# The operand stage of two memory attentions and of a latent attention put in another order

## The reference, cut to what matters

```python
def memory_xattn(h, mem_h, wq, wk, wv, wo):      # h: 512 x 1024, mem_h: 256 x 1024; 4 heads of 256
    q, k, v = h @ wq, mem_h @ wk, mem_h @ wv     # h = rmsnorm(x, xa_ln), mem_h = rmsnorm(mem, xa_mem_ln)
    p = softmax(q k^T * 256 ** -0.5)
    return (p @ v) @ wo

def _mla_queries(a_q, q_a_norm, w_uq, q_norm, rope):                 # a_q: 512 x 256
    q = (_rms_norm(a_q, q_a_norm) @ w_uq).reshape(B, L, 16, 96)
    q = _rms_norm(q, q_norm)                                         # per token and head
    return concatenate([q[..., :64], _rope_2d(q[..., 64:], rope)])

def _mla_keys_values(a_kv, kv_a_norm, w_ukv, k_norm, rope):          # 512 tokens of x, 256 of the context
    kv = (_rms_norm(a_kv[..., :128], kv_a_norm) @ w_ukv).reshape(B, L, 16, 64 + 64)
    k = _rms_norm(concatenate([k_nope, broadcast(k_pe)]), k_norm)    # per token and head
    return concatenate([k[..., :64], _rope_2d(k[..., 64:], rope)]), v
```

## Time and profile before

| | |
|---|---|
| median of 3 runs | 4220.62 us |
| the profiled execution | 4221.71 us |
| its span | 4219.7 us |
| TensorE busy | 3840.1 us (91%) |
| DVE, ACT, POOL busy | 1492.6 us, 1139.5 us, 99.4 us |
| mean granted TensorE clock | 0.954 of full speed |
| output product's end to scores, memory attention of layer 0 | 533.28 to 661.48 us |
| the same in layer 1 | 1625.2 to 1753.53 us |
| latent attention's operand block | 3405.2 to 3528.8 us |

### The profile page before, as it was taken

The page is one execution under the profiler, slowest core; times in us unless marked ns, Lnnn a source line. Parts: engine busy times, 40 slices in busy tenths (PEclk is TensorE's granted clock), DMA queues, the critical chain, the costliest instruction groups (busy, mean ns, idle before and its releaser), DMA issues. The chain is left out here.

```text
span 4219.7 us, 43015 instructions
## 1 busy us (share of the span) xinstructions
PE 3840.1 (91%) x17138; PEld 2784.8 (66%) x17138; DVE 1492.6 (35%) x2421; ACT 1139.5 (27%) x1932; POOL 99.4 (2%) x226
## 2 busy tenths in 40 slices
PE   7979789899999999989998999799999877887999
PEld 3447656678655885668784554488887744666777
DVE  2343313433302342243333333244433434544443
ACT  1122312322223442232232020221212424533222
POOL 0023000000000000000000000000000011000000
PEclk9979999999999999999999989899999988998999
DMA  3336222222311001212221201111112300001212
GB/s 132 115 121 224 101 90 79 80 95 84 113 60 40 1 1 70 100 60 99 82 98 66 70 19 40 40 40 60 60 51 99 132 20 21 1 31 69 80 70 99
DMA packets 29910, 307.53 MB, mean 73 GB/s; under 512 B 3715, under 2 KB 5476, under 8 KB 9029
## 3 DMA queue, kind: packets, MB, share of 16 engines
q1 hardware_dynamic: 29766, 305.52, 19.6%
HBM read 303.41 MB, written 2.10 MB: 72 GB/s over the span
## 5 line engine op out<-in xcount | busy, mean ns | idle before, releaser
L295 PE MATMUL psum<-h_all,ring 128*128 128x256 f32 (+2 forms) x2496 | 785.1, 474 | 16.9 <-DVE h_all L686 9.1
L295 PEld LDWEIGHTS psum<-h_all,ring 128*128 128x128 f32 (+1 forms) x2496 | 472.5, 190 | 322.9 <-issue 277.0
L523 PE MATMUL psum<-operand_rounded,weights_rest 128*128 128x512 f32 (+1 forms) x1360 | 520.6, 383 | 61.8 <-DVE operand_rest L494 61.8
L299 PE MATMUL psum<-operand_rounded,weights_rest 128*128 128x512 f32 x1216 | 488.8, 402 | 80.3 <-DVE weights_rest L318 80.3
L524 PE MATMUL psum<-operand_rounded,weights_rounded 128*128 128x512 f32 (+1 forms) x1360 | 517.6, 381 | 0.0
L525 PE MATMUL psum<-operand_rest,weights_rounded 128*128 128x512 f32 (+1 forms) x1360 | 516.5, 380 | 0.0
L301 PE MATMUL psum<-operand_rest,weights_rounded 128*128 128x512 f32 x1216 | 477.9, 393 | 0.0
L300 PE MATMUL psum<-operand_rounded,weights_rounded 128*128 128x512 f32 x1216 | 477.5, 393 | 0.0
L492 DVE TENSOR_TENSOR weights_rest<-ring,weights_rounded 128x1024 fp32r<-128x1024 f32 x170 | 208.2, 1225 | 572.9 <-ACT operand_rounded L476 572.9
L475 ACT ACTIVATE weights_rounded<-ring 128x1024 fp32r<-128x1024 f32 x170 | 179.9, 1058 | 630.5 <-PE psum L525 566.6
L523 PEld LDWEIGHTS psum<-operand_rounded,weights_rest 128*128 128x128 f32 x1360 | 260.7, 192 | 114.2 <-issue 55.4
(11 more groups left out here) (370 smaller groups left out, 4206.9 us busy)
## 6 DMA issues: line engine op xcount, KB each, us to landing
ring<-in_ff_w SPq DMA_DIRECT2D x32, 2048.0 KB, 7.8
ring<-in_w_mod SPq DMA_DIRECT2D x24, 2048.0 KB, 7.9
ring<-in_ffn_up SPq DMA_DIRECT2D x22, 2048.0 KB, 7.8
ring<-in_ffn_down SPq DMA_DIRECT2D x33, 1024.0 KB, 4.7
ring<-in_a_w_in SPq DMA_DIRECT2D x4, 2048.0 KB, 8.0
ring<-in_xa_wq SPq DMA_DIRECT2D x4, 2048.0 KB, 7.8
ring<-in_xa_wk SPq DMA_DIRECT2D x4, 2048.0 KB, 7.9
ring<-in_xa_wv SPq DMA_DIRECT2D x4, 2048.0 KB, 7.8
```

What stands on the lines that cost most here:

```text
L295: mm = nc.tensor.matmul(out, lhs, rhs, start=(t == 0), stop=(t == kt - 1))
L299: nc.tensor.matmul(out, rest, top_in, start=(t == 0), stop=False)
L523: nc.tensor.matmul(k.bank(m, n), rest, top_in, start=first, stop=False)
```

## The change

For the memory attentions:

- The memory is loaded during the output product before (`memory=True`), and the arena keeps its small size behind it, so that split parts fit beside it.
- One block, `cross_attention_operands`, replaces the three products. The order of the weights is keys, values, queries.
- DVE multiplies the memory by its gain only (eight ops of 128x256). TensorE multiplies the keys' and values' weights with that, in plain fp32 as before. The memory's inverse root is made meanwhile and put in where the results leave PSUM: DVE multiplies each key tile by the row of inverse roots; for the values, which have their tokens on partitions, the row is turned into a column by two one-row matmuls, and ACT copies with that scale.
- The query product runs last and split in three fp32r matmuls, with ACT rounding and DVE cutting x and each tile of 128 weight columns (two buffers).
- The final block of x's norm (DVE's scale and cut) stands behind the third key tile in DVE's list.

For the latent attention: DVE copies only group 1 of each key item, and does so between the mean and the guess's return; the two small mean ops become one (the factors 1/96 and EPS are put into `lat` and `pe_sum` once); the factor op becomes a tensor_tensor with a broadcast operand; queries(2) and queries(3) stand one turn earlier. Counters are renamed so that they are shared.

```diff
-def output_product(k, gate=None, norm=None):
+def output_product(k, gate=None, norm=None, memory=False):
     k.change_arena(SMALL_ARENA)
+    if memory:
+        k.load_later([(k.region(0, KT, MEM), k.dram["mem"])], "memory_landed")
     product_by_rows(k, k.h[:, :, 0:SEQ], gate, norm=norm)
-    k.change_arena()
+    if not memory:
+        k.change_arena()
...
-    product(k, "xa_wq", tokens, [(0, SEQ)], scalar=copy_out(k, lambda c, m, g: Q[:, 4 * c + m, :]), norm=norm)
-    product(k, "xa_wk", tokens, [(SEQ, MEM)], scalar=copy_out(k, lambda c, m, g: K[:, 4 * c + m, :]))
-    product(k, "xa_wv", tokens, [(SEQ, P), (SEQ + P, P)], stationary="tokens",
-            scalar=copy_out(k, lambda c, m, g: V[:, g, 512 * c:512 * c + 512]))
+    parts_scope, parts = k.place_parts()
+    cross_attention_operands(k, l, norm, mem, Q, K, V, parts)
...
+        def _(sp):
+            k.load_head(sp, wk, 2)
+            for w, done in ((wv, 4), (wq, 10)):
+                sp.wait_ge(*made.at(done))
+                k.load_chunk(sp, w, 0, slots[0])
+                sp.wait_ge(*made.at({4: 8, 10: 12}[done]))
+                k.load_chunk(sp, w, 1, slots[1])
+            sp.wait_ge(*made.at(16))
+            k.prefetch(sp, 1)
...
+        def _(pe):                  # six banks for the tiles in turn, bank 6 the sums, bank 7 the column
+            keys(0)                 # its first tile waits for gain_done
+            for t in range(KT):     # sums of the memory's squares
+                pe.wait_ge(*squared.at(t + 1))
+                mm = nc.tensor.matmul(k.bank(6, MEM), k.c("ones"), squares[:, t, :], start=(t == 0), stop=(t == KT - 1))
+            for n in range(1, 8):
+                keys(n)
+            pe.wait_ge(*v_step.at(3))
+            for g in range(2):
+                mm = nc.tensor.matmul(k.bank(7)[:, g:g + 1], rows[0:1, 2, g * P:(g + 1) * P], k.c("ones")[0:1, 0:1], start=True, stop=True)
+            for c in range(2):
+                for g in range(2):
+                    values(c, g)
+            for m in range(8):
+                queries(m)
...
+        def _(act):
+            # squares of the memory, Ln, Exp, Square of its mean; then
+            norm.guesses(act)
+            nc.scalar.activation(column, k.bank(7, 2), ACT.Copy).then_inc(column_copied.sem, 1)
+            copy_values(0, 0); copy_values(0, 1); round_weights(0)
+            copy_values(1, 0); round_weights(1); copy_values(1, 1)
+            for m in range(8):
+                if m + 2 < 8:
+                    round_weights(m + 2)        # waits until query tile m is made
+                copy_queries(m)
...
+        def _(dve):
+            # gained tiles, mean and two refining steps of the row; then
+            for n in range(8):
+                dve.wait_ge(*made.at(n + 1))
+                nc.vector.tensor_tensor(K[:, n, :], k.bank(n % TILE_BANKS, MEM), rows[:, 2], ALU.mult).then_inc(k_taken.sem, 1)
+                if n == 2:
+                    norm.scale(dve)
+            for m in range(8):
+                dve.wait_ge(*w_rounded.at(m + 1))
+                nc.vector.tensor_tensor(weight_part("rest", m), weight_tile(m), weight_part("rounded", m).bitcast(F32), ALU.subtract).then_inc(w_cut.sem, 1)
...
     def copied_by_act(i, q):
-        return not is_key(i) or q % 2 == 0
+        return not is_key(i) or q != 1
...
             queries(1)
+            queries(2)
             turn(6)
-            queries(2)
+            queries(3)
             turn(7)
-            queries(3)
             turn(8)
...
-                nc.vector.tensor_scalar(stat(i, 1), stat(i, 1), 1.0 / MLA_QK, EPS, ALU.mult, ALU.add).then_inc(mean.sem, 1)
+                if 1 <= i <= KB:
+                    copy_heads(i - 1)
                 dve.wait_ge(*item_act.at(3 * i + 3))
...
-                nc.vector.tensor_scalar(stat(i, 7), stat(i, 6), lat[:, 5, at:at + 1], None, ALU.mult).then_inc(item_dve.sem, 1)
+                nc.vector.tensor_tensor(stat(i, 7), stat(i, 6), lat[:, 5, at:at + 1].to_broadcast([P, H]), ALU.mult).then_inc(item_dve.sem, 1)
...
-XA = lambda l: [(f"xa_w{n}_{l}", KT, 512, 2) for n in "qkv"] + [(f"xa_wo_{l}", ROWS_OF_CHUNK, D, 2)]
+XA = lambda l: [(f"xa_w{n}_{l}", KT, 512, 2) for n in "kvq"] + [(f"xa_wo_{l}", ROWS_OF_CHUNK, D, 2)]
```

More of the change, by code:

```diff
@@ L1894, in pool_delta_layer @@
     mods.close()
-    output_product(k, norm=following)
+    output_product(k, norm=following, memory=True)
     return mods
[L1902 to L1908, removed]
 def cross_attention_layer(k, l, norm, following):
@@ L2067, in compressed_and_keys @@
     wide = lambda ap: ap.rearrange("p (h o) -> p h o", o=1).to_broadcast([P, NSA_HEADS, N_CMP])
-    made, taken = k.counter("nsa_tile_made"), k.counter("nsa_tile_taken")
+    made, taken = k.counter("operand_tile_made"), k.counter("nsa_tile_taken")
     biased, gated, pressed, second = (k.counter(n) for n in ("cmp_bias_made", "cmp_gates_made", "cmp_pressed", "cmp_second"))
@@ L3134, in _, with copy_heads @@
         def _(dve):
+            def copy_heads(i):
+                for q in range(4):
+                    if not copied_by_act(i, q):
+                        dve.wait_ge(*turned.at(4 * i + q + 1))
+                        dst, src = head_copy(i, q)
+                        nc.vector.tensor_scalar(dst, src, k_gain[0:MLA_QK], None, ALU.mult).then_inc(dve_copied.sem, 1)
             def total(i):
@@ L3166, in total @@
                 nc.vector.tensor_tensor(token_tile[:, i % 3, :, 0:d], tokens_psum(i), wide(stat(i, 7), d), ALU.mult).then_inc(scaled.sem, 1)
[L3168 to L3173, removed]
             dve.wait_ge(*sums_made.at(1))
@@ L3193, in _ @@
             dve.wait_ge(*lat_step.at(3))
-            nc.vector.tensor_tensor(lat[:, 6, :], lat[:, 5, :], lat[:, 5, :], ALU.mult).then_inc(lat_step.sem, 1)
+            nc.vector.scalar_tensor_tensor(out=lat[:, 6, :], in0=lat[:, 5, :], scalar=1.0 / MLA_QK, in1=lat[:, 5, :], op0=ALU.mult,
+                                           op1=ALU.mult).then_inc(lat_step.sem, 1)
             dve.wait_ge(*lat_step.at(4))
[L3196 to L3200, removed]
+            for i in range(ITEMS):
+                total(i)
         @block.gpsimd
@@ L3238, in mla_operands @@
     tables_landed.base += 32
-    for counter, steps in ((sums_made, 1), (pe_turned, 1), (means, 2), (guess, 3), (lat_step, 4), (raw_copied, 2), (pool_step, 8),
+    for counter, steps in ((sums_made, 1), (pe_turned, 1), (means, 2), (guess, 3), (lat_step, 4), (raw_copied, 3), (pool_step, 8),
                            (rotary_step, 3 * TT), (made, ITEMS), (squared, ITEMS), (totalled, ITEMS), (mean, ITEMS), (item_act, 3 * ITEMS),
-                           (item_dve, 5 * ITEMS), (scaled, ITEMS), (pe_filled, ITEMS), (v_made, KB), (v_copied, KB), (turned, 4 * ITEMS),
+                           (item_dve, 3 * ITEMS), (scaled, ITEMS), (pe_filled, ITEMS), (v_made, KB), (v_copied, KB), (turned, 4 * ITEMS),
                            (act_copied, act_copies[-1]), (dve_copied, dve_copies[-1])):
@@ L3294, in build @@
                  (k.x[:, :, SEQ:TOK], dram["ctx"])])
-        over_memory = [cross_attention_norm(k, l) for l in range(2)]
+        over_memory = [first_norm(k, "xa_ln", l) for l in range(2)]
         over_hidden = [first_norm(k, "ff_ln", l) for l in range(2)]
```

160 lines of the change are left out of this document (140 added, 20 removed).

## The result

The changed kernel takes 4163.57 us (median of 4 runs, 4160.03 to 4166.15) against 4221.17 (4 runs, 4220.14 to 4225.4): 57.6 us less, ratio 0.986 with a 95% interval of 0.9848 to 0.9872. The forecast was 4164. The profiled execution took 4160.03, 3.5 under its median, with a span of 4157.1; what the traces are made to explain is therefore 4221.71 - 4160.03 = 61.7 us.

The account below looks back on a forecast made before the run. TensorE, busy 91% of the span, was taken as the bound. Savings of 36.2 us in two memory attentions and 20.8 in the latent operands, together 57.0 off 4220.62, gave 4164; forecast 4158 to 4168, wider range 4152 to 4180.

Parts of the forecast that it names:

- The memory attention: Operand stage of each memory attention, norm boundary to scores: 106.3 us instead of 124.4, saving 18.1 a layer.
- the slow clock behind the gap: TensorE's clock after idling 4.2 us before the memory attention's keys: may fall, costing 2.0 us, bounds 0 and 4.
- First gained tile, column and boundary: Small terms on TensorE's path in the memory attention: 0.4 us, 0.4 us and 0.9 us.
- the covers: Memory attention: weight loads, rounding, cutting and DVE and ACT work stay hidden under TensorE's products; tightest had 3.6 us to spare.
- query chunk 0: Query weight load in the memory attention: needs 10.2 of 13.8 us with rounding and cutting, 3.6 us to spare.
- Rival C: Memory attention's split query product stays at half clock: 30 us slower than before, 4251 us; chance 0.02.
- The page against the row: Memory attention's split query product: 41.3 us by the skill page's four fp32 passes, 43.5 by the measured row, which was used.
- The queries of the latent stage: Latent attention's four query items, reordered: last turn starts at 39.7 us instead of 55.0 after queries(0), 15.3 saved.
- The keys: Latent attention's six key items: 5.5 us saved; 8.4 with the factor op free, 4.8 if held beside POOL in four.
- Rival D: More gain: the latent part keeps its clock up and the factor op is free, 4156 us; chance 0.14.
- Rival A: Latent key items: DVE's mid-chain stop for turned heads takes back the copies' gain, 4169 to 4172 us; chance 0.18.

## Why the prediction was right

**The total** is right for the reasons given, since each part came out near its own forecast by time, 34.0 for 36.2 and 23.6 for 20.8. That it is right within half a microsecond is luck: the two errors have opposite signs and cancel to 0.6, and in the traces too (34.3 for 36.2, 24.7 for 20.8).

**The memory attention: 107.2 us for 106.3.** The error is the sum of small ones. Keys and sums take 33.9 us from 539.68 to 573.58 for 33.4; in it the slow clock behind the gap, taken as 2.0, costs 2.7 (sixteen records in 6.22 us, which at 0.2177 are 3.5). The split product takes 44.1 for 43.5, since its first record (0.79) and its last don't lie under a neighbour. The value product takes 27.2 from its start to the next, 0.5 less than its row. First gained tile, column and boundary: 0.3 more together. All the covers held. The tightest, query chunk 0, is seen in ACT's timeline:

```profile
596.09 1.06 ACT L2046 ACTIVATE weights_rounded<-ring 128x1024 fp32r<-128x1024 f32 x1 [7.25 <-DMA ring<-in_xa_wq]
```

ACT waited 7.25 us for the chunk; the cut was ready at 598.4 and the queries began at 601.28: 2.9 us to spare, 3.6 forecast. ACT takes two query tiles 5.44 us apart at 640.01 and 645.45, the figure of the earlier trace rows to the digit.

**Rival C** (half clock in the split product) did not come: 1.00 throughout. The slow stretch ended after 6.2 us, within the first product, 55 us before the queries.

**The page against the row.** The Trainium skill's four passes for true fp32 (FP8 and Floating Point Precision, TensorE Precision Notes) would have put the split product at 41.3, an estimate; it took 44.1. Two records of 0.4305 us make one fp32 matmul, and one of the three that replace it takes 0.2267: 3.8 of these to one, and the saving is 20%, not 25%.

**The queries of the latent stage: 14.8 for 15.3.** Step by step behind the end of queries(0): queries(1) started at 6.65 (5.9 forecast), both products ended at 18.9 (18.1), queries(3) started at 20.9 (20.4), turn(9) at 40.3 (39.7). The first step was 0.75 late, and the later ones stayed 0.5 to 0.8 behind. As forecast, the last two rounds are bounded by POOL.

**The keys: 7.6 for 5.5.** Here is the step that failed. I had the factor op held beside POOL in four items, by the nearest row, one tensor_tensor with both inputs in SBUF that took 0.66 us. It was held in none; that makes 8.4 the right forecast and 7.6 the outcome. The kernel with the old form gives the term by itself: 4.0 us, four times 0.9 and a little. The row that misled me repeats in the new kernel (0.66 for 192 elements). I read it as an op beside POOL's; but it started 0.08 us behind POOL's op and ended 0.21 behind its end, while each factor op started ahead of POOL's. So the order of the two starts may have decided, or the size or the place of the op; no run tells them apart. The form decides as well, since the tensor_scalar was held although it too started first. The Trainium skill (GPSIMD Engine Reference, Specifications) names contention with two inputs in SBUF; here the small op of that kind ran in 0.17 us with POOL's op starting 0.04 behind it, and POOL's op took its usual 1.05, so the trace shows no cost on either side. What it says of the 2-port perf mode may fit the tensor_scalar that was held for 1.12, though no run here shows which mode an op used.

**What I left out: 2.3 us.** The old stage ended at a low clock, and the first scores paid for it: 4.92 us for eight matmuls, now 2.82. In the first 5.2 us of the attention the mean clock was 0.59, and is 1.00. I had counted the clock only inside the stage. With the keys' 2.1 more and the queries' 0.5 less it closes: 20.8 + 2.1 - 0.5 + 2.3 = 24.7, the trace's own figure, beside 23.6 by the medians.

**Rival D** (more gain, 4156) came true in half: the factor was free, but the clock from turn(5) to the scores was 0.77, little above the 0.72 of before.

**Rival A** (a stop in mid-chain takes back the gain) was priced at 4169 to 4172; the stop is there, DVE waits 6.3 us in four places for turned heads, but the chain of a key item had the room for one head. With two heads on DVE it came out as A describes, at 6.9 us.

## What to carry to other kernels

- Where TensorE stops and starts in turn, price a wait with what runs behind it: two waits cut by 2.6 us gave about 6, and an order of the same instructions with 7.6 us less of waits (12.6 for 20.2) gave 12.0. A wait of 4 us that became two of 1.24 and 1.50 no longer slowed the query products behind it; the two short waits themselves are still paid, and behind 1.81 and 1.02 us the value product still ran slowly (4.72 us for its eight records, 3.4 at full rate).
- Build the sum per stage from start-to-start distances and find among the moved transfers the one with the least room; here query chunk 0 had 2.9 us left of 13.8.
- In a serial chain of small ops beside a busy POOL, the form of a 0.2 us op can matter more than its work. Try the form by itself; a single row of a larger op does not tell, and note which engine's op started first in it.
- Compare a run's whole time with what its edited stretch explains. The kernels with the plain queries and with the late load were 17 and 5 us slower than their stages say, most of it at a lower clock in stretches that nobody had edited.

## What the runs showed of the hardware

- A tensor_scalar over 128x16 took 1.12 us when a 1.05 us op of POOL began 0.04 to 0.05 us behind its start, and 0.23 to 0.24 when that op began 0.11 behind or not at all. The tensor_tensor over the same elements took 0.17 to 0.18 in all ten cases, with POOL starting 0.04 behind it in some.
- The granted clock behind a gap: sixteen records that take 3.5 us at 2.4 GHz took 6.3 to 6.7 behind 4.3 us of idleness (both layers, all traces with the short gap) and 5.8 to 5.9 behind 8.86 to 9.07 us. Doubling the gap did not raise the loss.
- Behind waits of about 4 us a query product took 7.10 us, behind 0.25 us 5.32. Behind two waits of 1.24 and 1.50 us, half a turn apart, the two products took 10.46 for 24 records, close to the 10.33 of the full rate.
- An fp32 matmul with 512 columns took 0.861 us, one on rounded operands 0.2267 to 0.230 in a dense row of them.
- One stretch of layer 1's mixer, unedited in every kernel, took 67.9 to 68.0 us in ten traces, at a mean clock of 0.92, and 73.0 and 72.5 at 0.86 and 0.88 in the kernels with the plain queries and with the late load.
